# Two-layer streaming encoder step: the first RMS norm taken per token while loading, and the kept copy of x written in the DeltaNet stage

## What is computed

```python
def rmsnorm(x, g):
    y = x * lax.rsqrt(jnp.mean(x * x, -1, keepdims=True) + RMS_EPS)
    return y * g

hn = rmsnorm(x, norm_mix[i])          # i = 0: the norm of this change
y, cb, S = gated_deltanet(hn, ...)    # begins with hn @ w_in
x = x + y                             # x itself is needed again here
```

## Time and profile before

| what | us |
|---|---|
| three runs, median | 3348.61 (3344.56 to 3349.02) |
| the profiled execution | 3344.15 |
| its span, first to last instruction | 3342.1 |
| TensorE matmuls busy | 3108.6 (93%) |
| VectorE busy | 1513.0 (45%) |
| GpSimd busy | 1170.4 (35%) |
| ScalarE busy | 838.4 (25%) |

### The profile page before, as it was taken

How to read it: one execution, slowest core, us unless ns; L and a number is a source line. 1 busy time by engine, 2 the same in 40 slices (tenths; PEclk the granted TensorE clock), 3 DMA queues, 4 the chain that set the end, 5 groups by cost and what they waited for, 6 DMA issues and landing times. The chain is left out here.

```text
span 3342.1 us, 54213 instructions
## 1 busy us (share of the span) xinstructions
PE 3108.6 (93%) x19666; PEld 2988.9 (89%) x19666; DVE 1513.0 (45%) x3265; ACT 838.4 (25%) x1775; POOL 1170.4 (35%) x1005
## 2 busy tenths in 40 slices
PE   5988998899868999999999889999889999999998
PEld 4888888888858999999999789999789999999997
DVE  4566667666652433333333433333325333333334
ACT  2343443344342210111101224444422001110112
POOL 3323222322234543444434051222335344443430
PEclk7999999999979999999999999999889999999999
DMA  3100100010012111111111110101211111111101
GB/s 126 32 11 25 28 21 8 25 27 21 0 49 72 51 46 43 50 44 48 46 38 38 52 46 21 40 20 34 73 45 57 45 45 50 44 50 38 50 25 52
DMA packets 202973, 136.66 MB, mean 41 GB/s; under 512 B 32281, under 2 KB 192849, under 8 KB 202641
## 3 DMA queue, kind: packets, MB, share of 16 engines
q1 hardware_dynamic: 202896, 135.63, 13.8%
HBM read 120.98 MB, written 14.63 MB: 41 GB/s over the span
## 5 line engine op out<-in xcount | busy, mean ns | idle before, releaser
L92 PE MATMUL ps<-act_hi,w_hi 128*128 128x352 f32 x2328 | 799.6, 343 | 39.6 <-POOL w_lo L1625 20.7
L94 PE MATMUL ps<-act_hi,w_lo 128*128 128x352 f32 x2328 | 755.4, 324 | 0.0
L93 PE MATMUL ps<-act_lo,w_hi 128*128 128x352 f32 x2328 | 753.4, 324 | 0.0
L92 PEld LDWEIGHTS ps<-act_hi,w_hi 128*128 128x128 f32 x2328 | 442.5, 190 | 45.3 <-POOL w_lo L1625 21.3
L93 PEld LDWEIGHTS ps<-act_lo,w_hi 128*128 128x128 f32 x2328 | 443.9, 191 | 2.5
L94 PEld LDWEIGHTS ps<-act_hi,w_lo 128*128 128x128 f32 x2328 | 441.8, 190 | 0.0
L154 POOL TENSOR_TENSOR ffn_hi<-w_stage,one 128x512 fp32r<-128x512 f32 x200 | 208.9, 1045 | 656.8 <-PE ps L94 619.4
L92 PE MATMUL ps<-act_hi,ffn_hi 128*128 128x352 f32 x1344 | 435.4, 324 | 0.2 <-POOL ffn_lo L156 0.2
L93 PE MATMUL ps<-act_lo,ffn_hi 128*128 128x352 f32 x1344 | 431.5, 321 | 0.0
L94 PE MATMUL ps<-act_hi,ffn_lo 128*128 128x352 f32 x1344 | 431.5, 321 | 0.0
L154 POOL TENSOR_TENSOR w_hi<-w_stage,one 128x512 fp32r<-128x512 f32 x192 | 204.2, 1064 | 640.6 <-PE ps L94 337.8
(11 more groups left out here) (316 smaller groups left out, 4765.6 us busy)
## 6 DMA issues: line engine op xcount, KB each, us to landing
w_stage<-in_ffn_w_gu SPq DMA_DIRECT2D x88, 512.0 KB, 3.7
w_stage<-in_ffn_w_down SPq DMA_DIRECT2D x44, 512.0 KB, 3.5
w_stage<-in_gdn_w_in SPq DMA_DIRECT2D x32, 512.0 KB, 4.0
x_kept<-x SPq DMA_DIRECT2D x2, 4224.0 KB, 12.7
x<-x_kept SPq DMA_DIRECT2D x16, 528.0 KB, 4.1
load_rows<-in_x_prompt SPq DMA_DIRECT2D x8, 512.0 KB, 4.5
w_stage<-in_gdn_w_out SPq DMA_DIRECT2D x8, 512.0 KB, 3.9
w_stage<-in_ml_w_in SPq DMA_DIRECT2D x16, 256.0 KB, 4.5
```

The source lines that it names most:

```text
L92: pe.matmul(out, w_hi, rhs_hi, start=first, stop=False)
L93: pe.matmul(out, w_hi, rhs_lo, start=False, stop=False)
L94: return pe.matmul(out, w_lo, rhs_hi, start=False, stop=last)
```

## The change

The norm stage of layer 0 is no longer called. Its work is done in the load stage, on the rows as they arrive, tokens on the partitions: ScalarE squares a row tile and sums along the row in the same instruction, and makes the inverse root of one column; VectorE scales the rows by root and gain in one instruction; TensorE transposes both the rows (for `tk.x`) and the scaled rows (into banks 4 to 7); ScalarE rounds the scaled ones out of PSUM into `tk.hi`, VectorE subtracts to get `tk.lo`. All nine row tiles have buffers of their own. The gain is loaded once to all partitions, as SP's second DMA. The spill of x is issued by SP in the DeltaNet stage, behind weight block 1; ScalarE waits for it ahead of its first copy into `tk.x`.

```diff
-def load_phase(nc, tk, x_prompt, x_sample):
+def load_phase(nc, tk, x_prompt, x_sample, gain):
...
-        rows = buf("rows", [P, 3, D], F32)
+        rows = buf("rows", [P, TILES, D], F32)
+        normed = buf("normed", [P, 2, D], F32)
...
         @block.sync
         def _(sp):
             for c in range(TILES):
-                if c >= 3:
-                    sp.wait_ge(turned, 2 * (c - 2))
                 src = x_prompt[0, c * P:(c + 1) * P] if c < TILES - 1 else x_sample[0]
-                sp.dma_start(rows[0:size(c), c % 3], src).then_inc(landed[c % 3], 16)
+                sp.dma_start(rows[0:size(c), c], src).then_inc(landed[c], 16)
+                if c == 0:
+                    sp.dma_start(g[:], gain.rearrange("(a d) -> a d", a=1).to_broadcast([P, D])).then_inc(g_in, 16)
...
         @block.tensor
         def _(pe):
...
+            def normed_rows(c):
+                pe.wait_ge(normed_done, c + 1)
+                for half in range(2):
+                    if c >= 2:
+                        pe.wait_ge(lo_done, 2 * (c - 2) + half + 1)
+                    turn(normed[:, c % 2], c, half, 4 + c % 2 * 2 + half).then_inc(normed_turned, 1)
...
             for c in range(TILES):
...
+                    turn(rows[:, c], c, half, c % 2 * 2 + half).then_inc(turned, 1)
+                if c >= 1:
+                    normed_rows(c - 1)
+            normed_rows(TILES - 1)
+
+        @block.scalar
+        def _(act):
+            nc.scalar.preload_act_table_set("natural_log_exp_and_others")
...
+                nc.scalar.activation(sq[0:n], rows[0:n, c], ACT.Square, accum_out=r[0:n, c:c + 1]).then_inc(sq_done, 1)
+                act.wait_ge(sq_done, c + 1)
+                nc.scalar.activation(r[0:n, c:c + 1], r[0:n, c:c + 1], ACT.Ln, bias=tk.eps[0:n, 0:1],
+                                     scale=1.0 / D).then_inc(ln_done, 1)
+                act.wait_ge(ln_done, c + 1)
+                nc.scalar.activation(r[0:n, c:c + 1], r[0:n, c:c + 1], ACT.Exp, scale=-0.5).then_inc(r_done, 1)
+
+            def high(c):
+                for half in range(2):
+                    act.wait_ge(normed_turned, 2 * c + half + 1)
+                    nc.scalar.copy(columns(tk.hi, c, half), turned_rows(c, half, 4 + c % 2 * 2 + half)).then_inc(hi_done, 1)
+
+            act.wait_ge(made, 2)
+            for c in range(TILES):
+                root(c)
+                if c >= 2:
+                    high(c - 2)
+            high(TILES - 2)
+            high(TILES - 1)
 
         @block.vector
         def _(dve):
+            def scale(c):
+                n = size(c)
+                dve.wait_ge(r_done, c + 1)
+                if c >= 2:
+                    dve.wait_ge(normed_turned, 2 * (c - 1))
+                nc.vector.scalar_tensor_tensor(out=normed[0:n, c % 2], in0=rows[0:n, c], scalar=r[0:n, c:c + 1],
+                                               in1=g[0:n], op0=ALU.mult, op1=ALU.mult).then_inc(normed_done, 1)
+
+            def keep(c):
+                for half in range(2):
+                    dve.wait_ge(turned, 2 * c + half + 1)
+                    nc.vector.tensor_copy(columns(x, c, half), turned_rows(c, half, c % 2 * 2 + half)).then_inc(copied, 1)
+
+            def low(c):
+                for half in range(2):
+                    dve.wait_ge(hi_done, 2 * c + half + 1)
+                    nc.vector.tensor_tensor(columns(tk.lo, c, half), turned_rows(c, half, 4 + c % 2 * 2 + half),
+                                            columns(tk.hi, c, half).bitcast(F32), ALU.subtract).then_inc(lo_done, 1)
...
+            dve.wait_ge(g_in, 16)
             for c in range(TILES):
...
+                keep(c)
+                scale(c)
+                if c >= 2:
+                    low(c - 2)
+            low(TILES - 2)
+            low(TILES - 1)
+            dve.wait_ge(lo_done, 2 * TILES)
...
             sp.wait_ge(pro.w_split, 1)
-            for b in range(1, B):
+            weights(0, 0, 1)
+            sp.dma_start(tk.x_dram, tk.x[:]).then_inc(x_spilled, 16)
+            for b in range(2, B):
                 weights(0, 0, b)
...
                 silu(0, ch)
+                act.wait_ge(x_spilled, 16)
                 evacuate(0, 3 * NU + ch, True)
...
-        load_phase(nc, tk, a["x_prompt"], a["x_sample"])
-        norm_phase(nc, tk, a["norm_mix"][0], "norm0")
+        load_phase(nc, tk, a["x_prompt"], a["x_sample"], a["norm_mix"][0])
```

More of the change, by code:

```diff
@@ L354, in load_phase @@
         buf = lambda s, *a: ctx.enter_context(nc.sbuf_tensor(f"load_{s}", *a))
-        rows = buf("rows", [P, 3, D], F32)
-        landed = [sem(f"rows_landed{s}") for s in range(3)]
+        rows = buf("rows", [P, TILES, D], F32)
+        normed = buf("normed", [P, 2, D], F32)
+        g = buf("g", [P, D], F32)
+        sq = buf("sq", [P, D], F32)
+        r = buf("r", [P, TILES], F32)
+        landed = [sem(f"rows_landed{s}") for s in range(TILES)]
         made, turned, copied = sem("constants_made"), sem("turned"), sem("copied")
+        g_in, sq_done, ln_done, r_done = sem("gain_landed"), sem("sq_done"), sem("ln_done"), sem("r_done")
+        normed_done, normed_turned, hi_done, lo_done = (sem("normed_done"), sem("normed_turned"), sem("hi_done"),
+                                                        sem("lo_done"))
         block = ctx.enter_context(nc.Block())
@@ L422, in _, with columns, turned_rows, turn @@
                                              base=s - 1, pattern=[[2 * s, blocks], [0, s]], channel_multiplier=-1))
+        def columns(t, c, half):
+            return t[:, half * H:(half + 1) * H, c * P:c * P + size(c)]
+        def turned_rows(c, half, bank):
+            return ps[:, bank].rearrange("p (k t) -> p k t", k=H)[:, :, 0:size(c)]
         @block.tensor
         def _(pe):
+            def turn(src, c, half, bank):
+                for k in range(H):
+                    mm = pe.transpose(ps[:, bank, k * P:k * P + size(c)], src[0:size(c), (half * H + k) * P:(half * H + k + 1) * P],
+                                      tk.ident[0:size(c), 0:size(c)])
+                return mm
+            def normed_rows(c):
[4 more added lines that the diff above has]
+                    turn(normed[:, c % 2], c, half, 4 + c % 2 * 2 + half).then_inc(normed_turned, 1)
             pe.wait_ge(made, 5)
             for c in range(TILES):
-                pe.wait_ge(landed[c % 3], 16 * (c // 3 + 1))
+                pe.wait_ge(landed[c], 16)
                 for half in range(2):
@@ new lines, in _, with root @@
+                if c >= 1:
[4 more added lines that the diff above has]
+            nc.scalar.preload_act_table_set("natural_log_exp_and_others")
+            def root(c):
+                n = size(c)
+                act.wait_ge(landed[c], 16)
+                if c >= 1:
+                    act.wait_ge(sq_done, c)
+                nc.scalar.activation(sq[0:n], rows[0:n, c], ACT.Square, accum_out=r[0:n, c:c + 1]).then_inc(sq_done, 1)
[15 more added lines that the diff above has]
+            high(TILES - 1)
```

3 lines of the change are left out of this document (added).

## The result

The changed kernel took 3327.52 us in the median of four executions (3320.45 to 3330.11), the kernel before 3348.82 us beside it (four, 3344.56 to 3353.57): ratio 0.9934 with a 95% interval of 0.9916 to 0.9951, some 21 us less. A second series (in the experiments) gave 0.9952, 0.9938 to 0.9965, some 17 us less. The profiled execution took 3330.11 us over a span of 3328.4 us, where the kernel before had 3342.1.

What follows compares the result with a forecast made beforehand. The first 62 us, stages in sequence with barriers, delay everything behind; VectorE sets the new load stage. DeltaNet starts at 39.4 in place of 58.89, so 3344.15 - 19.5 = 3324.7 us, 3329 as median; range 3319 to 3339.

Steps and rivals of the forecast that it cites:

- VectorE sets the load stage: Load stage: VectorE's work per token tile, 3.81 us, exceeds ScalarE's 3.0 and TensorE's 1.7, so it sets the length.
- 3.81 us a tile: Load stage, VectorE per 128-token tile: two copies 1.29, scaling 1.27, two subtractions 1.25 us.
- The start at 5.9 us: Load stage: VectorE's first copy waits for the gain, which lands at 5.9 us, 1.25 behind the first tile's 4.63.
- TensorE's clock at 1.00 through the stage: Load stage: TensorE, about 45% busy, runs at 2.4 GHz throughout, its 16 transposes taking 1.7 us a tile.
- rival A: Load stage: TensorE at 1.2 GHz adds 0.8 to 2.8 us over eight tiles, time up to 3332; chance 0.16.
- Load end 38.8, DeltaNet stage 39.4: Load stage ends at 38.8 us; the DeltaNet stage starts 0.54 us later, at 39.4 in place of 58.89.
- First product 42.9: DeltaNet stage: TensorE's first product near 42.9 us, in place of 62.34.
- The half clock at the DeltaNet start stays as long: DeltaNet stage's start: TensorE's clock of 0.50 lasts as before, no gain; at best 2.7 us more.
- The spill costs nothing in its place: DeltaNet stage: the 4.2 MB spill behind weight block 1 costs nothing if it lands in 28 us, above that one for one.
- Rival C: DeltaNet stage: spill crawls beside weight loads, block 2 late, TensorE stands; slower by over 6.7 us from 54 us on; chance 0.03.
- Rival B: Load stage: two-tile lag fails, each tile one chain of 5.6 us, end at 54.2, time 3344, no change; chance 0.07.
- The sum: Whole kernel: 3344.15 less 19.5 gives 3324.7 us on the profiled execution's footing, 3329 us on the median's.

Runs made afterwards that it cites:

- the warm start: The changed kernel with 11 transposes of the identity on TensorE ahead of the first tile's rows and five ahead of the second's: 3326.87 us in one execution.
- the spill alone: The kernel before, norm stage kept, with only the spill of x moved to the DeltaNet stage behind weight block 1: ratio 0.9996, 3344.93 us beside 3346.61.
- the three spills: The changed kernel with three spills of x in a row in place of one, ScalarE waiting for all three: 3333.03 us in one execution.

## Why the prediction was right, point by point

- **VectorE sets the load stage:** shown. Twice the transposes change nothing in a tile (3.59 us), and one copy less makes it 2.99.
- **3.81 us a tile:** mis-sized; it was 3.59. The single durations were right (scaling 1.27, a copy or a subtraction 0.68 alone), but every operation overlaps its neighbour by about 0.08 us, scaling included, and not only those of a pair: 4 x 0.68 + 1.27 = 3.99, less 5 x 0.08. That was my lower bound (3.5), and I took the middle; eight tiles came 1.8 us shorter.
- **The start at 5.9 us:** it was 6.55. The gain took 5.2 us from issue to landing.
- **TensorE's clock at 1.00 through the stage:** wrong at its start, and at its end (1.94 us for the eight transposes at 33.54), where it cost nothing, as VectorE has no gap there. I weighed the Trainium skill's rule (TensorE: Matmul & The Clock Gate, section "The HAM clock gate": throttled by default, released by activity) against the clock column, which says 1.00 from the first microsecond, and took the column. The durations say otherwise, and one stood in my own rows: 32 transposes took 6.51 us at the start, 0.20 each, where eight took 0.14 each from 12.55 us on in the same trace (the line below). By the warm start the rule holds and the column is no reading there. The cost was rival A's in kind, 0.84 us of VectorE's waits and 1.07 us by the warm start, but in the first tiles only. At full clock, or with twice the work at it, the waits fit in.

```profile
12.55 1.09 PE L433 MATMUL ps<-ident,load_rows 128*128 128x128 f32 x8 [1.42 <-DMA load_rows<-in_x_prompt]
```

- **Load end 38.8, DeltaNet stage 39.4:** 38.4 and 38.9. That they came so close is partly luck: the too long tile (1.8 us) and the too early start with its slow transposes (0.65 + 0.84) mostly cancelled.
- **First product 42.9:** 43.31. GpSimd waited 1.55 us for the a/b weights (0.54 before); they took 3.3 us to land.
- **The half clock at the DeltaNet start stays as long:** it lasted 3.1 us in place of 5.4, a gain of 1.2 us or so that I had as the best case. A second fall behind a wait of TensorE of 1.77 us that ended at 58.51 (clock 0.66 from 60 to 65 us) took it back: block 1 to block 2 is 16.3 us here and 14.9 before, but 16.4 in the kernel with the spill alone, where the norm is as before, 16.5 in the second trace of the kernel before itself, and 14.9 with the transposes doubled. Eleven of the fourteen traces have this second fall; the first trace of before, the doubled transposes and the three spills have the same wait of 1.77 us and no fall behind it. What decides it stays open.
- **The spill costs nothing in its place:** shown by the spill alone, in its trace and with a ratio of 0.9996, and by the changed kernel, where nothing waits for it. The premise that a load behind it waits is shown by the landings of 12.6 and 30.4 us. The Trainium skill (DMA: Bandwidth & Descriptors, section "Queues, rings and completion order") says that an engine takes the descriptors of one queue in ring order, and these landings agree. Rival C's price was mis-sized: GpSimd wants block 2 at 28 us from issue, but TensorE only some 11 us later, so three spills cost 2.3 us of TensorE's waiting where my count says 14.
- **Rival B (one chain a tile, 5.6 us, an end at 54.2):** not what happened. Its price is about right, in part by luck: without the lag the next stage began at 54.35, but a tile took 5.06 us at the full clock for which I had worked out 5.6, and 5.75 at the half clock, which was no part of B.
- **The sum:** 3329 us forecast for the median, 3327.52 measured. At the stage's start 19.5 us were predicted and 20.0 found (19.7 against the second trace of before), at the first copy into x 18.7 (19.3), and 21 and 17 us in the medians of two series. On the footing of the profiled execution the same sum said 3324.7, and that execution took 3330.11: the first trace of before had the shortest rest of all fourteen, and two single spans compare no better than that.

## What to carry to other kernels

When a stage is folded into another, add up each engine's work in a tile and see that the written order leaves the others slack: here a lag of two tiles against none was worth 15.5 us, and the engine's own work only set the floor. A large transfer on a queue in order is placed by who stands behind it, counted to the engine that needs the data and not to the one that fetches them. A wait of TensorE can cost twice, as the wait and as a half clock behind it, though not after every wait (the one of 1.77 us in eleven of fourteen traces). Where it idles ahead of a stage, transposes that nobody reads brought its clock back earlier here, by 1.2 us at weight block 1, and kept up to the barrier they left no half clock at the stage's start.

## What the runs showed that was not expected

- The clock column says 1.00 in stretches at the start of a trace where transposes take twice their time (0.24 us each from 4.55 us on in the changed kernel, 0.13 later). Durations of one shape are the better clock there.
- VectorE's operations overlap their neighbours by 0.08 us even from one line to another, SBUF to PSUM (24.35 + 1.27 = 25.62, and the next starts at 25.54).
- The square's accumulator output is a separate ScalarE instruction of 0.19 us.
- The same code from the first copy into x to the end took 3223.6 to 3232.9 us in fourteen traces.
